# A modulation GEMV inside a fused two-block transformer kernel: one 256-row slice of its products is given to TensorE in quarters between matmul units, and the partition sums of a stage are made in one block with sixteen transposes behind them

## What is computed

```python
silu_c = jax.nn.silu(c)                                        # c: 1 x 2048
m_l = (silu_c @ ada_w[i] + ada_b[i]).reshape(bsz, 1, N_MOD, D_MODEL)      # ada_w: 2048 x 12288
n_l = modulate(rmsnorm(h_lat, norm_g[i, 0]), m_l[:, :, 0], m_l[:, :, 1])  # h*(1+scale)+shift
y_l = chunk_mlp_mix(n_l, a_w_in[j], a_g_v[j], a_w_s[j], a_b_s[j], a_w_out[j])
# chunk_mlp_mix: z = gelu(h @ w_in), w_in: 2048 x 8192; u, v = split(z)
```

## Time and profile before

| | before |
|---|---|
| time, median of 3 runs | 2316.41 us (2311.22 to 2317.02) |
| time of the profiled execution | 2314.73 us |
| its span in the trace | 2312.8 us (1.9 us less than its time) |
| TensorE busy | 2273.4 us, 98% of the span |
| TensorE's mean granted clock | 0.991 of full |
| first product of stages 0, 1, 2, 3 | 40.23, 73.16, 105.83, 138.51 us |

### The profile page before, as it was taken

How to read it: one execution, slowest core, us unless ns; L and a number is a source line. 1 busy time by engine, 2 the same in 40 slices (tenths; PEclk the granted TensorE clock), 3 DMA queues, 4 the chain that set the end, 5 groups by cost and what they waited for, 6 DMA issues and landing times.

```text
span 2312.8 us, 34482 instructions
## 1 busy us (share of the span) xinstructions
PE 2273.4 (98%) x13265; PEld 1987.5 (86%) x13265; DVE 1568.8 (68%) x2120; ACT 1135.5 (49%) x1700; POOL 103.1 (4%) x202
## 2 busy tenths in 40 slices
PE   6999999999999999999999999999999999999998
PEld 5788888888788888888888889999999999878987
DVE  6888777777788865666656767566566645655655
ACT  3355444444465543555445554444544444565544
POOL 0010100111100000000000001000000000100000
PEclk9899999999999999999999999999999999999999
DMA  9999788798867765555655565444444544544453
GB/s 368 387 378 400 236 284 265 243 332 314 304 221 249 251 198 193 182 182 185 197 181 198 186 197 168 151 155 139 142 148 144 164 149 161 169 135 125 139 183 127
DMA packets 230041, 493.05 MB, mean 213 GB/s; under 512 B 9682, under 2 KB 12520, under 8 KB 226824
## 3 DMA queue, kind: packets, MB, share of 16 engines
q1 hardware_dynamic: 210384, 432.05, 55.0%
q0 software_dynamic: 14272, 50.99, 6.6%
q10 hardware_dynamic: 5256, 8.20, 1.1%
HBM read 488.49 MB, written 2.10 MB: 212 GB/s over the span
## 4 chain that ended last, share of the span: by engine, by line
PE 85%; DVE 7%; DMA 5%; issue 2%; ACT 1%; SPq 0%; POOLq 0%; DVEq 0%; ACTq 0%
PE ps L1880 31%; PE ps L1927 22%; PE ps L1941 13%; PE ps L1943 7%; DMA ada<-in_ada_w 4%; PE ps L2417 4%; DVE acc L1195 2%; DVE wlo L1127 2%; PE ps L2240 1%; DVE acc L1136 1%; PE ps L2402 1%; PE ps L2259 1%; PE ps L2048 1%; DMA raw<-in_a_w_in 1%; PE ps L2386 1%
## 5 line engine op out<-in xcount | busy, mean ns | idle before, releaser
L1127 DVE TENSOR_TENSOR wlo<-raw,whi 128x1024 fp32r<-128x1024 f32 x720 | 872.6, 1222 | 501.7 <-ACT whi L580 500.2
L580 ACT ACTIVATE whi<-raw 128x1024 fp32r<-128x1024 f32 x720 | 756.5, 1057 | 807.7 <-PE ps L1880 393.4
L1941 PE MATMUL ps<-xt__59,whi 128*128 128x512 f32 x1408 | 498.4, 399 | 1.8 <-DVE h L1352 0.7
L1943 PE MATMUL ps<-xt__59,wlo 128*128 128x256 f32 x1408 | 395.4, 281 | 0.0
L1880 PE MATMUL ps<-whi,xt__59 128*128 128x512 f32 x1024 | 333.7, 403 | 7.0 <-DVE xt__59 L1269 7.0
L1941 PEld LDWEIGHTS ps<-xt__59,whi 128*128 128x128 f32 x1408 | 264.5, 188 | 69.2 <-DVE h L1352 2.2
L1927 PE MATMUL ps<-xmh__60,whi 128*128 128x272 f32 x1088 | 322.7, 297 | 0.6 <-DVE h L1352 0.3
L1927 PE MATMUL ps<-xmh__60,wlo 128*128 128x272 f32 x1088 | 314.9, 289 | 0.0
L1927 PE MATMUL ps<-xml__61,whi 128*128 128x272 f32 x1088 | 313.0, 288 | 0.0
L1943 PEld LDWEIGHTS ps<-xt__59,wlo 128*128 128x128 f32 x1408 | 266.0, 189 | 0.1
L1880 PEld LDWEIGHTS ps<-whi,xt__59 128*128 128x128 f32 x1024 | 198.3, 194 | 49.1 <-issue 7.4
(11 more groups left out here) (338 smaller groups left out, 3241.7 us busy)
## 6 DMA issues: line engine op xcount, KB each, us to landing
raw<-in_a_w_in SPq DMA_DIRECT2D x128, 1024.0 KB, 5.3
raw<-in_ffn_w_up SPq DMA_DIRECT2D x88, 1024.0 KB, 5.1
ada<-in_ada_w POOLq DMA_DIRECT2D x96, 512.0 KB, 4.7
raw<-in_a_w_out SPq DMA_DIRECT2D x48, 1024.0 KB, 5.9
raw<-in_ffn_w_down SPq DMA_DIRECT2D x44, 1024.0 KB, 5.1
mods<-in_ada_w SPq DMA_DIRECT2D x64, 512.0 KB, 11.0
raw<-in_b_w_in SPq DMA_DIRECT2D x32, 1024.0 KB, 5.5
ada<-in_ada_w SPq DMA_DIRECT2D x16, 1024.0 KB, 9.6
```

Source lines behind the costliest of these rows:

```text
L580: act.activation(whi[:, r % 4], raw[:, r // 2, r % 2], ACT.Copy).then_inc(hi_ready, 1)
L1127: dve.tensor_tensor(wlo[:, r % 4], raw[:, r // 2, r % 2], whi[:, r % 4].bitcast(F32), ALU.subtract).then_inc(lo_ready, 1)
L1941: pe.matmul(both, whi[:, r % 4, i, c * P:c * P + P], xt_[:, :, k * T:k * T + T], start=first and i == 0, stop=last and i == 1, skip_group_ ...
L1943: return pe.matmul(ps[:, bank + c, 0:T], wlo[:, r % 4, i, c * P:c * P + P], xth[:, k, :], start=False, stop=last and i == 1, skip_group_ch ...
```

## The change

Slice 2 instead of slice 3 goes to TensorE in stages 1 to 3. Its 16 matmuls are cut into four quarters, behind units 3, 4, 5 and 6 of the stage before (`COLUMN_AT`), where all 16 stood behind unit 6. `mod_last` sums the whole stage in one block into one bank, steps `mod_turned` once, and `mod_gain` runs once for all four tiles. In stages 1 to 3 `keep_warm` puts 16 transposes of the identity behind `mod_last`. Chunk 3 is now the first of a stage (`S_ORDER`), so its partial result is copied after unit 5's cast instead of after unit 7's; `LATE_LO` keeps its places relative to the slices that VectorE takes; in stage 3 the last partial sum is added at unit 4 instead of 7. `ADA4_AT` moves some of its 32 places. The sizes and number of all loads stay.

```diff
-PE_MOD = ((6,), (3,), (3,), (3,))
-S_ORDER = ((0, 3, 1, 2),) * 4
-LATE_LO = (0, 1, 2, 4)
+PE_MOD = ((6,), (2,), (2,), (2,))
+COLUMN_AT = {3: (0, 2), 4: (2, 4), 5: (4, 6), 6: (6, 8)}
+S_ORDER = ((3, 0, 1, 2),) * 4
+LATE_LO = (0, 1, 3, 4)
...
-def mod_columns(g, last=2):
+def mod_columns(g, last=True):
-    return 3 * g + 3 + last
+    return 2 * g + 3 + last
...
-                            sp.wait_ge(mod_turned, mod_columns(g0, 0))
+                            sp.wait_ge(mod_turned, mod_columns(g0, False))
...
-                    if i == 7 and g < 3:
-                        part_out(g, part3, 8 * g + 4)
+                    if i == 5 and g < 3:
+                        part_out(g, part3, 8 * g + 2)
...
+            def mod_gain(g):
+                n = len(PE_MOD[g]) + 1
+                dve.wait_ge(mod_turned, mod_columns(g))
+                own(dve.tensor_reduce(msum[:, :], ps[:, 6 + g % 2, 0:8 * n].rearrange("p (s m) -> p m s", m=8), AX.X, ALU.add))
...
-                    if g == 3 and i == 7:
-                        add_last(part3, 3, S_UNITS * 3 + 4)
+                        add_last(part3, 3, S_UNITS * 3 + 2)
...
-            def mod_column(g, d):
+            def mod_column(g, d, first=0, end=8):
...
-                for jb in range(8):
+                for jb in range(first, end):
...
-                mm.then_inc(mod_turned, 1)
+                if end == 8:
+                    mm.then_inc(mod_turned, 1)
+            def mod_last(g):
+                bank, s = 6 + g % 2, len(PE_MOD[g])
+                pe.wait_ge(mod_added, mod_adds(g, 7))
+                for jb in range(8):
+                    c0 = g * 512 + jb % 4 * P
+                    mm = pe.matmul(ps[:, bank, 8 * s + jb:8 * s + jb + 1], acc[:, jb // 4, c0:c0 + P], ones[:, 0:1],
+                                   start=True, stop=True)
                 mm.then_inc(mod_turned, 1)
...
                 mod_last(g)
+                if g:
+                    keep_warm(6 + (g + 1) % 2, 16)
...
-                    if u == S_UNITS * g + 6 and g < 3:
-                        pe.wait_ge(sem("part_copied"), 2 * (g + 1))
-                        mod_column(g + 1, 3)
+                    i = u - S_UNITS * g
+                    if i in COLUMN_AT and g < 3:
+                        if COLUMN_AT[i][0] == 0:
+                            pe.wait_ge(sem("part_copied"), 2 * (g + 1))
+                        mod_column(g + 1, 2, *COLUMN_AT[i])
```

More of the change, by code:

```diff
@@ L153, in at @@
     return G + t // 8, t % 8
-ADA4_AT = [(0, t) for t in (6, 8, 9, 10, 11, 13, 14)] + [(1, t) for t in (0, 1, 5, 6, 8, 9, 11, 12, 14, 15)]\
-    + [(2, t) for t in (0, 1, 5, 6, 7, 9, 10, 12, 13, 15)] + [(3, t) for t in (0, 1, 4, 5, 6)]
+ADA4_AT = [(0, t) for t in (6, 8, 9, 10, 11, 13, 14)] + [(1, t) for t in (0, 4, 5, 6, 8, 9, 10, 11, 12, 13, 14)]\
+    + [(2, t) for t in (0, 4, 5, 6, 8, 9, 10, 12, 13, 14)]\
+    + [(3, t) for t in (0, 4, 5, 6)]
 ADA5_OUT_AT = (7, 8, 9, 10, 11, 12, 13, 14)
@@ L683, in _ @@
                     cast(G_IN + u // 8, u % 8, g == 0)
-                act.wait_ge(sem("gain_n1"), 2 * g + 1)
+                act.wait_ge(sem("gain_n1"), g + 1)
                 for i in range(8):
@@ L695, in _ @@
                             act.wait_ge(sem("start_copied"), k // 2 + 2)
-                        if i:
-                            act.wait_ge(sem("gain_n1"), 2 * g + 2)
                         if i:
@@ L1198, in mod_group @@
                     between(d)
[L1200 to L1212, removed]
+            def mod_gain(g):
+                n = len(PE_MOD[g]) + 1
+                dve.wait_ge(mod_turned, mod_columns(g))
+                own(dve.tensor_reduce(msum[:, :], ps[:, 6 + g % 2, 0:8 * n].rearrange("p (s m) -> p m s", m=8), AX.X, ALU.add))
+                own(dve.tensor_tensor(mcol[:, 0:2, 4 * g:4 * g + 4], msum[:, :].rearrange("p (j b) -> p j b", b=4),
+                                      bcol[:, :, 4 * g:4 * g + 4], ALU.add))
+                dve.scalar_tensor_tensor(out=acol[:, 4 * g:4 * g + 4], in0=mcol[:, 1, 4 * g:4 * g + 4], scalar=1.0,
+                                         in1=cols[:, 16 + 4 * g:20 + 4 * g], op0=ALU.add, op1=ALU.mult)\
                    .then_inc(sem("gain_n1"), 1)
@@ L1253, in _ @@
                     lo(G_IN + u // 8, u % 8)
-                mod_gain(g, 0)
+                mod_gain(g)
                 for i in range(4 if g < 3 else S_UNITS):
@@ L1258, in _ @@
                         add_parts(part3, 1)
-                    if g == 3 and i == 7:
-                        add_last(part3, 3, S_UNITS * 3 + 4)
+                        add_last(part3, 3, S_UNITS * 3 + 2)
                     if i == 0:
-                        dve.wait_ge(sem("gain_n1"), 2 * g + 1)
+                        dve.wait_ge(sem("gain_n1"), g + 1)
                         dve.wait_ge(sem("start_copied"), 2 * g + 2)
@@ L1270, in _ @@
                            .then_inc(sem("nl"), 1)
-                    if i == 0:
-                        mod_gain(g, 1)
                     if i > 1:
@@ L1962, in keep_warm @@
                     pe.transpose(ps[:, bank, 384:512], ident[:, :], ident[:, :])
-            def mod_column(g, d):
+            def mod_column(g, d, first=0, end=8):
                 bank, s = 6 + g % 2, PE_MOD[g].index(d)
-                pe.wait_ge(mod_loaded[mod_slot(g, d)], mod_landed(g, d))
-                for jb in range(8):
+                if first == 0:
+                    pe.wait_ge(mod_loaded[mod_slot(g, d)], mod_landed(g, d))
+                for jb in range(first, end):
                     for i in range(2):
```

## The result

The changed kernel took 2329.27 us (median of 6 runs, 2326.90 to 2330.98); the kernel before, in the same comparison, 2315.57 us (6 runs). The ratio is 1.0062, with a 95% interval from 1.0049 to 1.0075: slower, by 11 to 17 us. Forecast were 2328.5 us, range 2322 to 2336, and slower with 0.89.

A forecast was written before the change was run, and what follows sets the result against it. TensorE, busy 98% of the span, bounds the kernel, with DMA near 32.5 us a stage early on; 16.1 - 3.1 = +13 us on 2314.73 gives 2327.7, from the median 2329.4; said 2328.5 us, range 2322 to 2336.

The forecast's parts named there:

- the slab path: Between stages: slice 7 and slab reach an empty queue in 8.0 us; slab landing to first product takes 5.26 us.
- the clock that comes back in part: Starts of stages 1 to 3: half of the 6.3 us lost to low clock given back, -3.1 us.
- from C to S: Column's end (C) to next stage's first product (S): 13.26 us, three times 39.8 against 23.7 before, +16.1 us.
- The wait that changed its place: SyncE's queue: slice 7, ahead of the slabs, now waits for TensorE's last quarter, so the DMA engines run dry.
- From S to C: Stage's first product to column's end, seven units and one column: quarters cost nothing, at most 1 us.
- Nothing different after the last stage: Expected sign in the changed trace: the work behind the last stage stays as it was.
- near 152: Expected sign: stage 3's first product near 152 us, 138.51 us before.
- Costs put at nothing: One gain and `mod_last`, chunk order, `part_out`, `LATE_LO`, stage 3 and `ADA4_AT`: nothing, the reordering and moves within 1 us.
- The DMA estimate: Load of 2 MiB to an empty queue: 8.2 us by the profile row, 6.8 us by the skill's figures.
- B: Rival: stages start slow, half clock lasts into the units and transposes are late, to +22 us; chance 0.15.
- C: As rival: shorter wait, queue refills faster and TensorE reaches its last quarter earlier, +4 to +9 us; chance 0.10.
- D: Rival: not slower, backlog covers the wait if the last quarter ends at least 5.7 us earlier; -7 us at most; chance 0.07.

The follow-up runs named there:

- experiment 1: Changed kernel with TensorE given slice 3 of stages 1 to 3 again and the remainders' old places, all else as changed: 2310.06 us, ratio 0.9990 to the kernel before.
- experiments 2: Kernel before with only slice 2 instead of slice 3 given to TensorE, in one piece behind unit 6: 2335.89 us, ratio 1.0104.
- 3 to 5: Changed kernel with the last small products behind unit 4, unit 5 or unit 7 instead of unit 6: ratios to before 1.0005, 1.0024 and 1.0100.
- experiment 6: Changed kernel without the 16 transposes behind `mod_last`: 2331.11 us, ratio 1.0078 to the kernel before.
- experiments 7 and 8: Changed kernel, respectively: slabs issued ahead of slice 7, ratio 1.0095; slice 3, small products behind units 4 to 6 and 8 transposes, ratio 0.9988.

## Why the prediction was right, and where its sum was off

The mechanism was right: the wait, the empty queue, the slab path, the clock that comes back in part. The total was right with luck: the term from C to S was 5.1 us too small, and a gain that the prediction didn't have, far behind the start, made up for most of it.

**The wait that changed its place: right.** SyncE reaches slice 7 at 52.5 us and waits to 65.27. Experiments 1 and 2 show this edit to be sufficient and necessary, 3 to 5 that the time follows the place of the last quarter. One reading was off: the queue was taken to be full up to the last landing, near 62.0 us. That load lands at 61.95, but the transfers fall from 340 GB/s (59.5 to 60 us) to 53 in the next half microsecond, so the load engines run nearly empty from 60.1 us on, 2 us earlier than the prediction had it.

**From C to S: 39.8 us were predicted for three stages, 44.9 measured** (80.05 - 65.24 = 14.81, 15.18, 14.95). The term that was mis-sized most is the transposes. VectorE's row that frees stage 1's first product in the changed kernel:

```profile
78.23 0.43 DVE L1264 TENSOR_TENSOR xt__59<-n1full,xt__59 128x256 fp32r<-128x256 f32 x1 [0.29 <-ACT xt__59 L701]
```

It ends at 78.66, and in experiments 2 and 6 TensorE starts 0.13 us behind such a row. So without transposes in the way the first product could have come at 78.79, C + 13.55; in the same way at C + 13.9 and C + 13.7 in stages 2 and 3. It came 1.2 to 1.3 us later each time, 3.7 us in all, behind transposes that were put at up to 0.7 us late and at nothing in the middle of the forecast. They end last, at C + 14.8 to 15.2, because they start late and both blocks run at the low clock, 3.57 + 3.5 us. They start late because of a wait that I had wrong: I let VectorE add the first half of slice 7 while the second was in flight. Both halves step one semaphore and `mod_group` waits for both, so both additions, 2 x 1.30 us, come after the second landing (70.62 us; the first half had landed at 69.2). The additions were to end at C + 6.6 and end at 73.27 - 65.24 = C + 8.0.
The other 1.4 us are in the path itself, C + 13.55 to 13.9 instead of 13.26: the slab lands 7.1 + 0.96 = 8.1 us after C in stage 1, as predicted, but with the late additions the sums end just behind the remainder (76.88 and 76.78 us), and the gain waits for both. In experiments 2 and 6 the slab lands 8.2 to 9.6 us after C, and the 5.26 us from its landing to the first product come out to 0.02 us wherever the slab is last; in stage 1 of experiment 6 it is the sums that are last. So C - S was +21.2 us (44.94 - 23.74) instead of +16.1.

**From S to C and the clock: -3.1 us predicted, -3.9 measured.** From S to C it took 25.03, 24.00 and 23.21 us, 72.2 against 74.5 before: -2.3 us. In this the quarters cost something and the clock gives something. Stage 3's units now start at clock 1.00, where the 20 us from 138 us had 0.91 before. By the clock, 0.09 x 20 = 1.8 us came back there, and unit 32's remainder, which VectorE made 157.3 us into the kernel before, came 17.3 us later, 1.6 less than the 18.9 of stage 3's first product. So the share that came back was over half of the 6.3 us once the transposes ran, though they themselves ran at half clock. In experiment 6, without the transposes, the stages' units took 0.6 and 2.6 us longer, and each first product took 0.77 us, the time at the low level; so the transposes are what brought the units of stages 2 and 3 to the high level from their second product on.
The Trainium skill (TensorE: Matmul & The Clock Gate, "HAM oscillation — how this bites in real kernels") says that an array which waits for DMA in each round starts each round at the low clock. The 0.50 of the three stretches from 73.4, 112.5 and 150.7 us agrees.

**What came back later was not predicted.** "Nothing different after the last stage" was one of the signs named, and it failed: 13.5 us of span are left of 17.3. The rest, 3.7 us, comes back in one part: the up-projection of the feed-forward block. A 60 us stretch of it in the kernel before and after:

```profile
700.00:760.00 60.00, 60.00 (x342) 52.01 (x341) 49.43 (x58) 31.57 (x37) 4.51 (x9) 1.00 0.80 276
...
717.00:777.00 60.00, 60.00 (x348) 52.91 (x347) 50.00 (x59) 33.13 (x39) 4.22 (x8) 1.00 0.79 272
```

At the same clock of 1.00 and no idle time TensorE made 348 matmuls instead of 342; 60 / 342 - 60 / 348 = 3.0 ns each, over the 1024 matmuls of that part 3.1 us (the whole part took 4.1 us less, 656.03 to 833.73 us against 638.33 to 820.14, and 0.4 us had been lost ahead of it). The change doesn't touch this work. Had this pace been the same in both, the profiled difference would have been about 17 us. So the forecast of 13 us met the profiled 13.5 by luck: its own terms, measured, make 17.3 at the end of the start, and the first product of stage 3 came at 157.4 us where "near 152" was named. The timed difference of 13.7 us (11 to 17) may hold the same luck or not; no run tells.

**Costs put at nothing.** One gain instead of two, the order of the chunks and the moved additions: experiment 1 holds them all, with quarters and transposes, at 0.9990 [0.9974, 1.0006]. Together, with what the clock gives back, they are not above 0.06% and not told apart. The one that had been missed in them is the wait of the first quarter for a slice that hasn't landed, and it exists only with slice 3.

**The DMA estimate.** The row gave 8.2 us for 2 MiB to an empty queue. In the changed kernel it took 73.3 - 65.27 = 8.0 us in stage 1, of which 0.93 passed before SyncE issued the slab.
The estimate after the Trainium skill (DMA: Bandwidth & Descriptors, "Anatomy of one DMA — SWDGE (gpsimd) path") was 6.8 us, 1.2 less than measured. That section's figures are for one load from GpSimd's queue, and these are three from SyncE's, so the run doesn't tell which part of them is short here.

**Rivals.** B (to +22) was near in its cause, late transposes, and wrong in its effect, since the units did not start slower. C fails on both of its conditions: 2 MiB took 8.0 us and not less than in the rows, and the last quarter in stage 0 ended at 65.24 us, not ahead of 64.94; SyncE waited 12.7 us each time on average, where some 11 were expected. The "+7.5" that the range takes as C's middle is above the middle of its +4 to +9, 6.5; the lower end would be 1 us less, which changes nothing here. D's point of decision was put at 5.7 us earlier than unit 6, and 2.8 us ahead of the queue's end. With the last quarter behind unit 4, 5.05 us earlier (65.24 - 60.19), the ratio is 1.0005, but the start is still 6.4 us late in the profiled execution: the backlog doesn't cover the whole wait there.

## What to carry to other kernels

In a ring of buffers that is filled by one queue in written order, ask of each slot who frees it and what stands behind that wait in the queue: giving another piece of work to an engine that comes to it late moves the wait to another load, here from behind 4 MiB of slabs to ahead of them, at 38 us of waiting and 14 us of time, with not one load more. The backlog gives the deadline. Here two units earlier, at 60.2 us, took away most of the loss and not all of it; between units 5 and 7 each us later cost a us in each round. Count it from where the transfers run down (60.1 us), which is 2 us ahead of the last landing. When a queue has run dry, what counts is the whole chain behind the late load, and filling the queue with other loads in the meantime lengthened it (10.34 us instead of 4.94).

## What the runs showed of the hardware

**Two paces at full clock.** The up-projection's matmuls (512 and 256 columns by turns) ran in each profile of this study at one of two paces. Before, in experiments 1 and 2 and with the last quarter behind unit 5 it was the slower one, in the changed kernel and with units 4 and 7 the faster one. In the version without transposes, and in those of experiments 7 and 8, the pace changed within the execution, from the faster to the slower, at a stop of 0.9 to 1.3 us. Two stretches of the first and the stop between them:

```profile
660.00:700.00 40.00, 40.00 (x233) 35.01 (x232) 36.98 (x55) 27.55 (x37) 2.11 (x4) 1.00 0.59 198
720.00:760.00 40.00, 40.00 (x228) 34.72 (x227) 32.41 (x39) 21.20 (x25) 3.17 (x6) 1.00 0.81 284
...
716.60 0.50 PE L1934 MATMUL ps<-xt__59,whi 128*128 128x512 f32 x1 [1.26 <-DVE wlo L1127]
```

233 and 228 records in 40 us with no idle time and clock 1.00 in both, 171.7 and 175.4 ns each by the records. Over the whole part the two paces are about 4 us apart (177.6 and 181.8 us, above), which is part of the spread between executions of a kernel (2303.55 to 2314.95 us in experiment 1). What sets the pace stays open; nothing here tells whether the change has a part in it.

**A switch to one-column products costs.** In the changed kernel's timeline the unit behind a quarter:

```profile
53.27 0.94 PE L1965 MATMUL ps<-ccol,mods 128*128 128x1 f32 x8
54.08 0.49 PE L1873 MATMUL ps<-whi,xt__59 128*128 128x512 f32 x1
54.41 0.40 PE L1873 MATMUL ps<-wlo,xt__59 128*128 128x512 f32 x1
54.64 0.63 PE L1873 MATMUL ps<-whi,xt__59 128*128 128x512 f32 x2
```

The second matmul starts 0.33 us after the first, the third 0.23 after the second, and the chain of the kernel has 2.89 us for each of these units of 12 matmuls, against 2.72 (12 x 0.2267) for those with no small products ahead. Not all of it is the price of cutting a column up, since a column in one piece has such a unit behind it too. A quarter and its unit take 3.68 us from start to start (53.27 to 56.95), four times (3.68 - 2.72) is 3.8 us a column. In one piece it took 3.49 us (93.92 to 97.41, before), and with the same 0.15 us in the unit behind it 3.6. So each of the three further pieces costs an estimated 0.06 us.
